# Differential attention with the scores of both maps in two row groups of TensorE, PSUM tiles of its own, and a deeper lag between scores and values

## The chip, the cores and the metric

One core of a Trainium2 chip runs the whole program. The metric is the device time of one execution in microseconds (us). TensorE (PE) multiplies, VectorE (DVE) and ScalarE (ACT) work on its results, GpSimd (POOL) and SyncE (SP) serve around them.

## What is computed

Two layers of a hybrid backbone over 256 context and 512 latent tokens. Each layer has three groups of heads (an SSD scan, differential attention, latent attention) behind one input projection, and then a mixture of 16 experts. The change is in the differential attention: four heads, each with two maps of 32 dimensions and values of 64.

```python
s1 = jnp.einsum('bqhd,bkhd->bhqk', q1, k1).astype(F32) * scale
s2 = jnp.einsum('bqhd,bkhd->bhqk', q2, k2).astype(F32) * scale
amap = jax.nn.softmax(s1, axis=-1) - lam * jax.nn.softmax(s2, axis=-1)
o = jnp.einsum('bhqk,bkhd->bqhd', amap.astype(v.dtype), v)
return rmsnorm(o, subln_w) * (1.0 - lambda_init)
```

Context queries see the 256 context keys, latent queries all 768. In layer 0 there are 2 context and 4 latent query tiles of 128 for each head, in layer 1 only the 4 latent ones.

## The kernel before

The work of the stage is cut into units, one for each head and query tile: 24 in layer 0 (8 with 256 keys, 16 with 768) and 16 in layer 1 (all with 768 keys). Everything is float32. Every engine has its own program, written out in order, and waits on semaphores; nothing is rearranged. Of each float32 matmul the trace shows two instructions, of a transpose one.

`QK` holds queries (rows m = 0, 1) and keys (m = 2, 3) with 128 partitions: four groups of 32, which are heads 2m and 2m+1, each with its two maps. To take one map alone out of the 128 partitions, ScalarE copies the queries with a mask (`split_queries`, line 821) into `QS`, so that the other 96 partitions are zero; a score matmul then runs over all 128 rows (`diff_score`, line 1568 in `scores`).

A unit on PE is (`attention`): scores of the *next* unit, both maps (512 and 256 key columns each); the transposes of this unit's weighted map, 128 columns each (`turn_tile`, line 1553); the values of the unit before (line 1579, 64 columns). VectorE (`attend`) takes the negative row maximum of each map (line 1061), combines the two exponentials (lines 1145 to 1151: the second map times its factor, added to the first) and scales the result (line 1155). ScalarE (`softmax`) computes the exponentials with their row sums (line 775) and copies the transposed map out of PSUM (line 696). The latent attention later in the layer uses the same `attention`, `softmax` and `attend` with one map.

PSUM is four tiles of 1024 columns, `ps[0]` to `ps[3]`, two banks each. Everything up to the experts goes through numbered jobs (`job_plan`, `att_job`, class `Slots`): job j uses tile j mod 4 when the job four before it has been released. The differential attention has 4 jobs for each unit (two scores, one turn, one value).

Behind the stage PE goes on with the projection for the latent attention (line 1545, 352 columns), and with the matmuls of the modulation. The latent attention's own projections use narrow matmuls: lines 1704 and 1705 (128 and 64 rows by turns, 96 columns), 1716 (32 rows and columns), 1722 (128 rows, 64 columns). In the SSD stage lines 1778 and 1812 multiply in two groups of 64 rows, into different PSUM banks.

```python
    scores(0)
    for u in range(n):
        if u + 1 < n:
            scores(u + 1)
        pe.wait_ge(*w_.next(S["prob_ready"]))
        turn_tile(...)
        if u:
            values(u - 1)
    values(n - 1)
```

## Time and profile before

| | us |
|---|---|
| median of 3 runs | 2569.79 (2564.29 to 2576.02) |
| the profiled execution | 2569.09 |
| its span on the core | 2567.3 |
| stage in layer 0, first score to last finish (146.17 to 250.35) | 104.18 |
| stage in layer 1 (1479.81 to 1561.16) | 81.35 |
| mean granted TensorE clock | 0.892 |

The profile comes from one execution. Each instruction has a start and a duration; an idle stretch is shown with the instruction that ended it. PE's matmuls are pipelined, so the duration of one is longer than its share of the engine: distances between starts tell the price. PEclk is the clock that TensorE was granted, as a share of full speed; in this trace it is at any moment either 0.50 (1.2 GHz) or 1.00 (2.4 GHz). The two stages are 7.2% of the time; the expert stages, 4 out of 10 slices and more, stream weights and are not touched.

### The profile page before, as it was taken

Reading aid. Unit: us, or ns where it says so; the run is one execution under the profiler, and the core shown is the slowest. Engines: PE = TensorE matmul, PEld = TensorE weight load, DVE = VectorE, ACT = ScalarE, POOL = GpSimd, SP = SyncE. Lnnn points to the kernel's source line nnn. Section 1 sums busy time; section 2 is a strip of 40 time slices with the busy share of each in tenths; the row PEclk is TensorE's granted clock in tenths of the full one; section 3 lists DMA queues with packets and bytes.
Section 4 is the critical chain, followed back from the end, with each engine's and each line's share of the span. In section 5 each row is a group of like instructions: output and inputs, shape, how many; then the busy total and the mean of one; then the engine's idle time right before and its main releaser. Section 6 shows DMA issues by size and latency. Waiting matters only on the chain. (4 is left out here: it accounts for less than half of the span.)

```text
span 2567.3 us, 26052 instructions
## 1 busy us (share of the span) xinstructions
PE 2187.0 (85%) x11014; PEld 1161.4 (45%) x11014; DVE 659.5 (26%) x1161; ACT 520.6 (20%) x1040; POOL 214.6 (8%) x187
## 2 busy tenths in 40 slices
PE   4898999988894999999994999999879587777774
PEld 2466456657452333333332776466544332222221
DVE  1156142127334111111103163322372400000001
ACT  3144243131230000000004252332212000000001
POOL 0000000023001111111100000000220000000000
PEclk8899889897985999999997999798869698888887
DMA  8400403100033999999996002231001599999995
GB/s 297 148 34 1 164 1 116 66 33 1 0 115 128 381 396 396 396 395 397 400 386 220 33 34 73 92 116 64 36 1 73 209 402 402 402 402 402 402 403 208
DMA packets 168647, 527.78 MB, mean 206 GB/s; under 512 B 10584, under 2 KB 24532, under 8 KB 168404
## 3 DMA queue, kind: packets, MB, share of 16 engines
q1 hardware_dynamic: 155412, 494.65, 49.6%
q0 software_dynamic: 11680, 26.22, 4.0%
q10 hardware_dynamic: 1440, 5.24, 0.5%
q8 instruction: 88, 1.44, 0.2%
q14 instruction: 27, 0.22, 0.0%
HBM read 503.02 MB, written 23.07 MB: 205 GB/s over the span
## 5 line engine op out<-in xcount | busy, mean ns | idle before, releaser
L1927 PE MATMUL ps<-ring,arena 128*64 128x512 f32 x1184 | 287.6, 640 | 56.7 <-DMA ring<-in_w_up 44.5
L1927 PE MATMUL ps<-arena 128*64 128x512 f32 x864 | 210.3, 640 | 42.5 <-DMA arena<-in_w_up 29.3
L1536 PE MATMUL ps<-arena,ring 128*128 128x256 f32 (+1 forms) x640 | 203.5, 481 | 12.3 <-DMA ring<-in_w_in 12.3
L1545 PE MATMUL ps<-ring,arena 128*128 128x256 f32 (+3 forms) x736 | 207.8, 444 | 0.0
L1927 PEld LDWEIGHTS ps<-ring,arena 128*64 128x64 f32 x1184 | 93.5, 147 | 236.4 <-issue 236.4
L696 ACT ACTIVATE arena<-ps 128x768 f32<-128x768 f32 (+8 forms) x143 | 106.9, 758 | 325.9 <-PE ps L1545 150.0
L1545 PEld LDWEIGHTS ps<-ring,arena 128*128 128x128 f32 x736 | 138.7, 215 | 67.5 <-issue 44.0
L1536 PEld LDWEIGHTS ps<-arena,ring 128*128 128x128 f32 x640 | 122.7, 192 | 92.1 <-issue 83.4
L1553 PE MATMUL ps<-const,arena 128*128 128x128 f32 x732 | 110.7, 297 | 57.9 <-ACT arena L742 38.1
L1568 PE MATMUL ps<-arena 128*128 128x256 f32 (+3 forms) x432 | 151.4, 485 | 7.6 <-ACT arena L775 4.0
L1927 PEld LDWEIGHTS ps<-arena 128*64 128x64 f32 x864 | 68.1, 147 | 173.5 <-issue 173.5
L1477 DVE TENSOR_TENSOR arena<-arena,ps 128x512 f32<-128x512 f32 x32 | 22.0, 688 | 460.4 <-ACT arena L983 460.4
L1848 PE MATMUL ps<-ring,arena 128*128 128x512 f32 x320 | 138.9, 593 | 1.1 <-DVE arena L1362 1.1
L1981 PE MATMUL ps<-ring,arena 128*64 128x512 f32 x608 | 136.8, 595 | 3.0 <-DMA ring<-in_w_down 2.3
L1553 PEld LDWEIGHTS ps<-const,arena 128*128 128x128 f32 x732 | 93.9, 155 | 80.7 <-ACT arena L742 39.7
L606 POOL DMA_INDIRECT expert_sums<-arena,small x32 | 52.8, 1650 | 865.6 <-ACT arena L990 825.1
L775 ACT ACTIVATE arena<-ps,nmax 128x768 f32<-128x768 f32 (+1 forms) x120 | 97.1, 812 | 131.4 <-DVE nmax L1061 124.7
L1061 DVE TENSOR_REDUCE nmax<-ps 128x1 f32<-128x768 f32 (+1 forms) x120 | 98.5, 846 | 69.9 <-PE ps L1568 69.9
L983 ACT ACTIVATE arena<-ps 128x512 f32<-128x512 f32 x32 | 19.1, 597 | 448.0 <-PE ps L1927 448.0
L1579 PE MATMUL ps<-arena 128*128 128x64 f32 x832 | 105.3, 277 | 0.0
L1579 PEld LDWEIGHTS ps<-arena 128*128 128x128 f32 x832 | 102.9, 199 | 0.0
L1568 PEld LDWEIGHTS ps<-arena 128*128 128x128 f32 (+1 forms) x432 | 75.9, 191 | 58.9 <-issue 50.9
(227 smaller groups left out, 2358.8 us busy)
## 6 DMA issues: line engine op xcount, KB each, us to landing
ring<-in_w_up SPq DMA_DIRECT2D x38, 2048.0 KB, 17.7
ring<-in_w_down SPq DMA_DIRECT2D x38, 2048.0 KB, 23.9
ring<-in_w_gate SPq DMA_DIRECT2D x36, 2048.0 KB, 22.5
arena<-in_w_gate SPq DMA_DIRECT2D x28, 2048.0 KB, 23.1
arena<-in_w_up SPq DMA_DIRECT2D x26, 2048.0 KB, 16.0
arena<-in_w_down SPq DMA_DIRECT2D x26, 2048.0 KB, 24.9
ring<-in_ada_w SPq DMA_DIRECT2D x24, 2048.0 KB, 13.2
ring<-in_w_in SPq DMA_DIRECT2D x6, 2048.0 KB, 9.8
```

The lines of the kernel that those rows point to most:

```text
L606: pool.indirect_dma_start(halves_sum[l], at_rows(e, 0), y_l[e % 2], None, compute_op=ALU.add)\
L696: act.activation(dst, src, func, scale=scale).then_inc(*J.free(j))
L775: act.activation(P_of[i % 2][m][:, 0:nk], J.tile(j)[:, 0:nk], ACT.Exp, bias=nmax[:, c:c + 1], accum_out=esum[:, c:c + 1]).then_inc(*J.free(j))
L1061: dve.tensor_reduce(nmax[:, c:c + 1], J.tile(j)[:, 0:nk], AX_X, ALU.max, negate=True).then_inc(S["negmax"], 1)
L1536: ins = mm(o[0:n, c0:c1], w[:, k, col:col + n], hT[:, k, c0:c1], start=k == 0, stop=k == KD - 1)
L1545: ins = mm(o[:, i * stride:i * stride + n], hT[:, k, t * P:(t + 1) * P], w[:, k, :], start=k == 0, stop=k == KD - 1)
L1553: ins = pe.transpose(o[:, k * P:(k + 1) * P], src(k), ident)
L1568: ins = mm(o[:, c0:c1], lhs, rhs, start=True, stop=True)
L1579: ins = mm(o[:, 0:64], PT_of[u % 2][:, k * P:(k + 1) * P], v_of(h, k), start=k == 0, stop=k == nk - 1)
L1848: ins = mm(o[:, hf * 512:(hf + 1) * 512], mixT[i % 2][:, k, :], wo[hf][:, k, :], start=k == 0, stop=k == KD - 1)
L1927: ins = mm(ps[0][hf * 64:hf * 64 + 64, col:col + 512], xl[e % 2][:, at:at + CAP_L], w[:, c, hf * 512:hf * 512 + 512], start=b + c == 0, st ...
L1981: ins = mm(ps[1][hf * 64:hf * 64 + 64, 512:1024], hT_l[e % 2][:, at:at + CAP_L], w[:, c, hf * 512:hf * 512 + 512], start=b + c == 0, stop= ...
```

## The change

- The masked copies and `QS` are gone. A score matmul reads 32 rows: `r` picks the row group of the head and map in `QK`, for queries and keys alike. For each span of keys the two maps follow each other, so two neighbouring matmuls stand in neighbouring row groups and write different PSUM tiles.
- The stage no longer uses the job numbering. Its scores rotate over `ps[0]` to `ps[2]` (index 2u + m modulo 3), so scores of unit u need the first exponential of unit u-1. `ps[3]` serves the rest: three transposes at a time in its first bank, the values in its second. (The number of jobs removed is a multiple of 4, so later jobs keep their tiles.)
- A tile of 768 keys is transposed and copied in two halves of 3 x 128 columns. A half waits until ScalarE has copied the one before.
- The lag is deeper: in round r PE does scores of r, then by turns halves of the transposes of r-2 and of the values of r-3. `P1` has three buffers, `P2` and `PT_d` two each, `rcol` four sets.
- Each engine has a loop of its own for the stage: `diff_softmax` on ScalarE, a loop with `diff_max`, `diff_weigh`, `diff_finish` on VectorE, and one with `diff_scores`, `diff_turn`, `diff_values` on PE. Their arithmetic is as before.

```diff
+def diff_parts(l):
+    return [(u, k, min(k + 3, n_keys(t) // P)) for u, (h, t) in enumerate(diff_units(l)) for k in range(0, n_keys(t) // P, 3)]
...
-        PD = [[ar(a2 + (2 * i + m) * TOK, TOK) for m in range(2)] for i in range(2)]
-        PT_d = [ar(a2 + (4 + i) * TOK, TOK) for i in range(2)]
-        QS = view(ar(a2 + 6 * TOK, 4 * TOK), m=4)
+        P1 = [ar(a2 + i * TOK, TOK) for i in range(3)]
+        P2 = [ar(a2 + (3 + i) * TOK, TOK) for i in range(2)]
+        PT_d = [ar(a2 + (5 + i) * TOK, TOK) for i in range(2)]
...
+                for r in range(n + 2):
+                    for m in range(2):
+                        if r >= 2:
+                            turned_out(r - 2, m)
+                        if r < n:
+                            exps(r, m)
...
-                        act.activation(QS[:, i, tq:TOK], QK[:, h // 2, tq:TOK], ACT.Copy,
-                                       scale=K[:, K_MAP + i:K_MAP + i + 1]).then_inc(S["q_split"], 1)
...
+                for r in range(n + 3):
+                    if r < n:
+                        diff_max(r, 0)
+                        diff_max(r, 1)
+                    if 1 <= r <= n:
+                        diff_weigh(r - 1)
+                    if r >= 3:
+                        diff_finish(r - 3)
...
-                def diff_score(h, m, t, c0, c1):
-                    if t == q[0] and c0 == 0:
-                        pe.wait_ge(*w_.next(S["q_split"]))
-                    return QS[:, 2 * (h % 2) + m, t * P:(t + 1) * P], QK[:, 2 + h // 2, c0:c1]
-
-                attention(l, DH, jb("datt"), 2, diff_score, PD, PT_d, lambda h, k: V[:, k, h * DV:(h + 1) * DV])
+                def diff_scores(u):
+                    h, t = units[u]
+                    if u >= 2:
+                        pe.wait_ge(S["diff_exps"], 2 * (n0 + u) - 1)
+                    elif u == 1:
+                        pe.wait_ge(S["diff_exps"], 2 * n0 + 1)
+                    for c0, c1 in spans(t):
+                        for m in range(2):
+                            r = slice(32 * (2 * (h % 2) + m), 32 * (2 * (h % 2) + m) + 32)
+                            ins = mm(ps[(2 * u + m) % 3][:, c0:c1], QK[r, h // 2, t * P:(t + 1) * P], QK[r, 2 + h // 2, c0:c1],
+                                     start=True, stop=True)
+                            if c1 == n_keys(t):
+                                ins.then_inc(S[f"diff_scored{m}"], 1)
+                def diff_turn(u, x):
...
+                    pe.wait_ge(S["diff_weighed"], n0 + u + 1)
+                    if i:
+                        pe.wait_ge(S["diff_copied"], p0 + i)
+                    for k in range(k0, k1):
+                        ins = pe.transpose(ps[3][:, (k - k0) * P:(k - k0 + 1) * P], P1[u % 3][:, k * P:(k + 1) * P], ident)
+                    ins.then_inc(S["diff_turned"], 1)
...
+                for r in range(n + 3):
+                    if r < n:
+                        diff_scores(r)
+                    for x in range(2):
+                        if 2 <= r < n + 2:
+                            diff_turn(r - 2, x)
+                        if r >= 3:
+                            diff_values(r - 3, x)
```

How PE's program reads now, at two places. The names are PSUM tile <- operands, then the shape; x3 is a count of matmuls in a row.

The start of the stage in layer 0, before: scores of line 1568 for units 0, 1 and 2, transposes of line 1553 between them.

```order
L1568 MATMUL ps1<-arena 128x256
L1568 MATMUL ps2<-arena 128x256
L1568 MATMUL ps3<-arena 128x256
L1568 MATMUL ps0<-arena 128x256
L1553 MATMUL ps1<-const,arena 128x128 x2
L1568 MATMUL ps2<-arena 128x512
L1568 MATMUL ps2<-arena 128x256
L1568 MATMUL ps3<-arena 128x512
L1568 MATMUL ps3<-arena 128x256
```

And now, where line 1740 is the scores and line 1754 the transposes.

```order
L1740 MATMUL ps0<-arena 128x256
L1740 MATMUL ps1<-arena 128x256
L1740 MATMUL ps2<-arena 128x256
L1740 MATMUL ps0<-arena 128x256
L1740 MATMUL ps1<-arena 128x512
L1740 MATMUL ps2<-arena 128x512
L1740 MATMUL ps1<-arena 128x256
L1740 MATMUL ps2<-arena 128x256
L1754 MATMUL ps3<-const,arena 128x128 x2
L1740 MATMUL ps0<-arena 128x512
```

Three units' scores (256, 256, then 512 and 256 keys) stand ahead of the first transpose, and the maps alternate within a span.

A latent unit of the same layer, before: scores of line 1568, six transposes, six values of line 1579.

```order
L1568 MATMUL ps2<-arena 128x512
L1568 MATMUL ps2<-arena 128x256
L1568 MATMUL ps3<-arena 128x512
L1568 MATMUL ps3<-arena 128x256
L1553 MATMUL ps0<-const,arena 128x128 x6
L1579 MATMUL ps1<-arena 128x64 x6
```

And now, with the values in line 1768.

```order
L1740 MATMUL ps1<-arena 128x512
L1740 MATMUL ps2<-arena 128x512
L1740 MATMUL ps1<-arena 128x256
L1740 MATMUL ps2<-arena 128x256
L1754 MATMUL ps3<-const,arena 128x128 x3
L1768 MATMUL ps3<-arena 128x64 x3
L1754 MATMUL ps3<-const,arena 128x128 x3
L1768 MATMUL ps3<-arena 128x64 x3
```

The scores are as many, the transposes and values come in threes by turns, all of them in `ps3`.

## Rows read from the trace of the kernel before

**Rows 1.** Page, first line and part 1: busy us, share of span, instructions

```profile
span 2567.3 us, 26052 instructions
...
PE 2187.0 (85%) x11014; PEld 1161.4 (45%) x11014; DVE 659.5 (26%) x1161; ACT 520.6 (20%) x1040; POOL 214.6 (8%) x187
```

**Rows 2.** Busy time by windows, both stages: stretch, us, PE, PEld, DVE, ACT, POOL, PEclk, DMA

```profile
146.17:250.35 104.18, 91.69 (x497) 68.16 (x498) 69.17 (x144) 55.25 (x124) 0.00 (x0) 0.98 0.06 21
1479.81:1561.16 81.35, 77.40 (x417) 58.87 (x418) 54.90 (x96) 43.83 (x84) 0.00 (x0) 0.96 0.08 27
```

**Rows 3.** Timeline, one latent unit of layer 1: start, us, engine, line, operation, shape

```profile
1520.10 2.80 PE L1568 MATMUL ps<-arena 128*128 128x512 f32 x8
...
1522.11 1.82 DVE L1061 TENSOR_REDUCE nmax<-ps 128x1 f32<-128x768 f32 x2
...
1522.73 0.82 PE L1553 MATMUL ps<-const,arena 128*128 128x128 f32 x6
1523.15 0.90 ACT L775 ACTIVATE arena<-ps,nmax 128x768 f32<-128x768 f32 x1 [0.79 <-DVE nmax L1061]
...
1523.39 1.45 PE L1579 MATMUL ps<-arena 128*128 128x64 f32 x12
...
1524.68 1.51 PE L1568 MATMUL ps<-arena 128*128 128x512 f32 x4
...
1524.92 0.81 ACT L696 ACTIVATE arena<-ps 128x768 f32<-128x768 f32 x1
```

**Rows 4.** Timeline of PE, three places at line 1778, 64-row matmuls

```profile
557.53 0.28 PE L1788 MATMUL ps<-const,arena 128*128 128x128 f32 x1
557.74 0.38 PE L1778 MATMUL ps<-arena 64*128 64x128 f32 x2
...
570.91 0.49 PE L1778 MATMUL ps<-arena 64*128 64x128 f32 x4 [0.16 <-ACT arena L922]
571.34 0.49 PE L1787 MATMUL ps<-const,arena 128*128 128x128 f32 x2
...
586.86 0.80 PE L1778 MATMUL ps<-arena 64*128 64x128 f32 x4
587.59 0.79 PE L1787 MATMUL ps<-const,arena 128*128 128x128 f32 x2
```

**Rows 5.** Windows again: stretches before, in and after half clock

```profile
243.40:246.60 3.20, 1.65 (x15) 1.65 (x16) 1.40 (x3) 1.20 (x2) 0.00 (x0) 1.00 0.02 5
...
1550.40:1553.90 3.50, 1.91 (x18) 1.77 (x16) 2.34 (x6) 2.57 (x5) 0.00 (x0) 1.00 0.01 2
1554.20:1560.60 6.40, 6.31 (x30) 6.32 (x31) 0.31 (x2) 0.81 (x1) 0.00 (x0) 0.50 0.01 3
298.02:322.36 24.34, 24.34 (x32) 6.27 (x32) 0.00 (x0) 2.42 (x3) 0.00 (x0) 0.50 0.47 174
322.36:331.03 8.67, 8.67 (x12) 1.56 (x11) 6.41 (x8) 0.81 (x1) 3.31 (x4) 0.50 0.00 0
...
335.40:342.00 6.60, 5.91 (x23) 3.38 (x21) 0.76 (x2) 3.92 (x5) 0.00 (x0) 1.00 0.00 0
1609.20:1626.80 17.60, 17.51 (x32) 6.30 (x32) 0.00 (x0) 1.78 (x3) 0.00 (x0) 0.50 0.63 232
...
1564.20:1572.00 7.80, 7.80 (x28) 5.05 (x27) 1.43 (x5) 0.16 (x2) 0.00 (x0) 1.00 0.00 0
```

**Rows 6.** Timeline of PE at half clock: transposes, values, 32-row and 64-column matmuls

```profile
1554.29 1.54 PE L1553 MATMUL ps<-const,arena 128*128 128x128 f32 x6 [1.98 <-DVE arena L1151]
1555.62 5.22 PE L1579 MATMUL ps<-arena 128*128 128x64 f32 x24
1560.63 1.49 PE L1545 MATMUL ps<-ring,arena 128*128 128x352 f32 x2
...
322.36 8.74 PE L1716 MATMUL ps<-arena,const 32*32 32x512 f32 x10
331.03 7.50 PE L1722 MATMUL ps<-arena,w_kv_up 128*64 128x512 f32 x16
```

More of the change, by code:

```diff
@@ L148, in job_plan, with diff_units, diff_before, diff_parts_before @@
     return at
+def diff_units(l):
+    return [(h, t) for h in range(DH) for t in query_tiles(l)]
+def diff_before(l):
+    return sum(len(diff_units(i)) for i in range(l))
+def diff_parts(l):
+    return [(u, k, min(k + 3, n_keys(t) // P)) for u, (h, t) in enumerate(diff_units(l)) for k in range(0, n_keys(t) // P, 3)]
+def diff_parts_before(l):
+    return sum(len(diff_parts(i)) for i in range(l))
 def att_job(base, maps, n, u, kind, m=0):
@@ L760, in conditioning, with diff_softmax, exps, turned_out @@
                 modulation(l, 0)
+            def diff_softmax(l):
+                units, parts, n0, p0 = diff_units(l), diff_parts(l), diff_before(l), diff_parts_before(l)
+                n = len(units)
+                def exps(u, m):
+                    nk, c = n_keys(units[u][1]), 2 * (u % 2) + m
+                    act.wait_ge(*a.next(S["negmax"]))
+                    if m == 0:
+                        if u >= 3:
+                            act.wait_ge(S["diff_turned"], p0 + len([p for p in parts if p[0] <= u - 3]))
+                        if u >= 2:
+                            act.wait_ge(S["diff_weighed"], n0 + u - 1)
+                    act.activation((P1[u % 3] if m == 0 else P2[u % 2])[:, 0:nk], ps[(2 * u + m) % 3][:, 0:nk], ACT.Exp,
+                                   bias=nmax[:, c:c + 1], accum_out=esum[:, c:c + 1]).then_inc(S["diff_exps"], 1)
+                def turned_out(u, x):
+                    mine = [(i, p) for i, p in enumerate(parts) if p[0] == u]
+                    if x >= len(mine):
+                        return
+                    i, (_, k0, k1) = mine[x]
+                    if x == 0 and u >= 2:
+                        act.wait_ge(S["diff_valued"], n0 + u - 1)
+                    act.wait_ge(S["diff_turned"], p0 + i + 1)
+                    act.activation(PT_d[u % 2][:, k0 * P:k1 * P], ps[3][:, 0:(k1 - k0) * P], ACT.Copy)\
+                        .then_inc(S["diff_copied"], 1)
+                for r in range(n + 2):
[4 more added lines that the diff above has]
+                            exps(r, m)
             def softmax(l, heads, base, maps, P_of, PT_of, after_exps=None):
@@ L1140, in _, with diff_max @@
                     dve.wait_ge(*v.next(S["qk_roped"]))
[L1142 to L1145 removed]
+                units, n0 = diff_units(l), diff_before(l)
+                n = len(units)
+                def diff_max(u, m):
+                    nk, c = n_keys(units[u][1]), 2 * (u % 2) + m
+                    dve.wait_ge(S[f"diff_scored{m}"], n0 + u + 1)
+                    if u >= 2:
+                        dve.wait_ge(S["diff_exps"], 2 * (n0 + u - 2) + m + 1)
+                    dve.tensor_reduce(nmax[:, c:c + 1], ps[(2 * u + m) % 3][:, 0:nk], AX_X, ALU.max,
+                                      negate=True).then_inc(S["negmax"], 1)
@@ new lines, in _ @@
+                n = len(units)
+                def diff_scores(u):
+                    h, t = units[u]
+                    if u >= 2:
+                        pe.wait_ge(S["diff_exps"], 2 * (n0 + u) - 1)
[8 more added lines that the diff above has]
+                                ins.then_inc(S[f"diff_scored{m}"], 1)
@@ new lines, in diff_turn @@
+                def diff_turn(u, x):
+                    mine = [(i, p) for i, p in enumerate(parts) if p[0] == u]
+                    if x >= len(mine):
+                        return
+                    i, (_, k0, k1) = mine[x]
+                    pe.wait_ge(S["diff_weighed"], n0 + u + 1)
[4 more added lines that the diff above has]
+                    ins.then_inc(S["diff_turned"], 1)
@@ new lines, in diff_values @@
+                def diff_values(u, x):
+                    h, t = units[u]
+                    mine = [(i, p) for i, p in enumerate(parts) if p[0] == u]
+                    if x >= len(mine):
+                        return
+                    i, (_, k0, k1) = mine[x]
+                    pe.wait_ge(S["diff_copied"], p0 + i + 1)
+                    if x == 0 and u:
+                        pe.wait_ge(S["diff_finished"], n0 + u)
+                    last = n_keys(t) // P
+                    for k in range(k0, k1):
+                        ins = mm(ps[3][:, 512:512 + DV], PT_d[u % 2][:, k * P:(k + 1) * P], V[:, k, h * DV:(h + 1) * DV],
+                                 start=k == 0, stop=k == last - 1)
+                    if k1 == last:
+                        ins.then_inc(S["diff_valued"], 1)
```

51 lines of the change are left out of this document (24 added, 27 removed).

## The prediction

> **What bounds the kernel now.** TensorE is busy 85% of the span [rows 1], so I first cut out the two stretches that hold the changed stage, by stage windows: layer 0 takes 104.18 us with PE busy 91.69, layer 1 81.35 us with PE busy 77.40, the clock at 0.98 and 0.96 of full; the queue of work behind them is PE's next projection, so what they gain or lose goes into the total one to one [rows 2]. Then the order in time of one steady unit (layer 1, a latent tile with 768 keys) [rows 3]: scores start at 1520.10, transposes at 1522.73, values at 1523.39, the next scores at 1524.68. That is 2.63 + 0.66 + 1.29 = 4.58 us with PE never waiting; 16 units make 73.3 of the 81.35 us. VectorE is busy 54.90/16 = 3.4 us and ScalarE 43.83/16 = 2.7 us a unit [rows 2]. PE is the bound, at the full clock of 2.4 GHz.
>
> **The change part by part.**
>
> *Scores by row groups.* Each matmul of the scores now reads 32 rows, and the two maps stand in neighbouring row groups and in different PSUM tiles. The nearest row is the pair of 64-row matmuls of line 1778: four take 0.43 us from load to the next full-array load (570.91 to 571.34), and the first two together span 0.38 us, one lone full-array matmul and a load of 0.1 us (0.28 at 557.53) [rows 4]. So pairs do run side by side. For a latent unit this makes 2.56 us of streams (2.63 less the first load) into 1.28 us.
>
> *Going in and out of row groups.* Full-array matmuls of 128 columns follow each other 0.11 us apart (six transposes in 0.66 us [rows 3]), but line 1788 to line 1778 takes 0.21 us, and a visible load of about 0.1 us follows; four 64-row matmuls should stream in 2 x 0.11 us and take 0.43, so 0.2 us goes on the way out [rows 4]. One visit costs 0.4 us at the full clock; at half clock 0.73 less 2 x 0.21 leaves 0.3, plus the turn-in and its load again 0.3: 0.6 us. Bounds are 0.3 and 0.6 there. I take 0.6, since the stage visits just as line 1778 does, between full-array work.
> The rule for this stands in the Trainium skill, "TensorEngine Tiling (Array Packing)", Key Properties: a change of tiling mode drains the engine. The trace agrees with 0.2 us each way; a sum that left it out would be 24 us lower for 40 visits.
>
> *PSUM and order.* Three score tiles instead of four slots: scores of unit u wait for the first exponential of unit u-1. Before, the first two units' scores stood in a row; now each of the first rounds is scores, a wait for maximum and exponential, scores. Behind the waiting scores stand the transposes of u-2 and values of u-3, and ScalarE's copy of them. Copies by halves: 0.81 us for 768 columns becomes two of about 0.5 (an estimate between zero saving and twice 0.81), on ScalarE, which has 1.9 us free. The masked copies of line 821 (8 in all, about 0.7 to 0.9 us each) go from ScalarE; they hid behind PE, so nothing is won. The VectorE work is the same.
>
> *Would the loop hold 4.58 at full clock?* Scores to availability 0.2 + 1.28 + 0.27, maximum 0.95 (two in 1.82), ScalarE ready only after the half copy of the tile turned in between (about 0.15 late), exponential with its accumulator 1.0: 3.9 us a unit. PE's own sum is 1.28 + 0.4 + 0.66 + 1.29 = 3.63, so that loop would be the bound. It would still be a gain. But it needs 2.4 GHz.
>
> **The clock decides.** What the engine did before its clock fell: 1.65 us of work in 3.20 (243.4 to 246.6), and 1.91 in 3.50 (1550.4) [rows 5]; both are waits for VectorE in the stage's own tail, and both are followed by half clock, 1.2 GHz. The new stage opens like that: in layer 1 its first two rounds each hold 1.5 us of score matmuls in a round of about 3.6 us (latencies as above), and these fill 64 of the 128 rows. I expect the clock to fall there, in both layers.
>
> Before, full-array work brought it back: after some us of line 1545, which begins at 1560.63 [rows 6], the clock is 1.00 from 1564.2 [rows 5]. In the new stage two kinds of work alternate, and each has a row in which a busy PE did **not** bring it back [rows 5]. Matmuls on 64, 96 or 128 rows by turns and then on 32 rows (lines 1704, 1705, 1716) fill PE without a gap from 298.02 to 331.03, 33 us, and again from 1609.20, and the clock is 0.50 throughout; behind them the 128-row matmuls of line 1722, which begin at 331.03 [rows 6], raise it (1.00 from 335.4). Transposes and values (lines 1553, 1579) fill 6.31 of 6.40 us from 1554.20 at 0.50. PE being busy was not enough in either. With scores on 64 of 128 rows and transposes and values between them I expect the clock to stay at 0.50 to the stage's end.
> The Trainium skill, "TensorE: Matmul & The Clock Gate", What's actually happening, says that activity releases the throttle, and its advice is to keep PE busy without long gaps. By that alone a PE with 3.63 us of work in 3.9 is safe; that is rival A below, 2554 us. The 33 us above speak against it.
>
> **The sum at half clock.** Prices by rows at 0.50: ten 32-row matmuls of 512 columns in 8.67 us (322.36 to 331.03), 0.86 each; six transposes in 1.33 us (1554.29 to 1555.62, 0.16 of it a first load), so about 0.213 each; 24 value instructions in 5.01 us (1555.62 to 1560.63), 0.209 each [rows 6]. A latent unit: scores 2 x 0.86 + 2 x 0.43 = 2.58, visit 0.6, transposes 6 x 0.213 = 1.28, values 12 x 0.209 = 2.51: 7.0 us. PE is then far behind every other engine and hides all their waits.
> Layer 0: scores 16 x 2.58 + 8 x 0.86 = 48.2; visits 24 x 0.6 = 14.4; 112 transposes 23.9; 224 value instructions 46.8; sum 133.3. Opening and tail: before, 81.35 - 73.3 = 8 us in layer 1; now a round more at the front, less what the first 5 us at full clock save. I take 9 here and 6 in layer 1. Layer 0: 142.3, **+38.1**.
> Layer 1: 16 x 2.58 + 16 x 0.6 + 96 x 0.213 + 192 x 0.209 = 111.4, with 6: 117.4, **+36.1**.
> The profiled execution took 2569.09 us (span 2567.3 and 1.8 around it), 0.7 below the median of three, 2569.79. 2569.1 + 74.2 = **2643 us**. Bounds: visits at 0.3 take 12 off, opening and tail give or take 8, projection still at half clock after the stage adds up to 4.
>
> **Rivals.**
> A. *The clock holds* (it never falls, or comes back within some us). Units of 3.9 us: layer 1 16 x 3.9 + 9 = 71, layer 0 16 x 3.9 + 8 x 3.2 + 6 = 94, and 3 us in each for one dip at the start or end: 97 and 74, so -7 and -7: **2554 us** (2549 to 2560). For it: PE's gaps stay short, 0.98 now. Against: rows 5. Chance 0.13.
> B. *The clock falls and comes back now and then*, for example at the context tiles, where full-array work of older units stands closer together: half way, about **2600 us**. Chance 0.10.
> C. *The row groups run one after the other*, since each float32 matmul is two instructions and the second pass could block the neighbour. Then scores double at half clock, +48 and +41 on the above: **2732 us**; at full clock units of 4.6 to 5.0 and +18, 2587. Against: line 1778 is float32 too, and its pairs lie together [rows 4]. Chance 0.05.
> The side on which it turns slower: from about 15% of the stage at half clock on, the 15 us of rival A are eaten (a unit at half clock costs 3.1 us more; 5 of 40 units do it).
>
> **How the numbers follow.** Forecast 0.72, A 0.13, B 0.10, C 0.05. The predicted time is the forecast's. The range takes it with its bounds (2620 to 2672) and B: 2575 to 2675, 0.81. About 0.5% (13 us) is what a measurement of this kernel can tell from no change; faster by more is most of A, 0.10; within it the rest of A and the edge of B, 0.04; slower 0.86.
>
> **What would show it.** The granted clock of the two stretches: 0.5 and a stage of about 142 and 117 us, against 0.95 and 97 and 74. Score matmuls in pairs that start together, four pairs in 2.6 us at half clock; a unit of 7.0 us in layer 1; VectorE and ScalarE waiting for PE. Elsewhere every stage should last as long as before. I am wrong if the clock treats two maps side by side as it treated the full-array scores, if the opening is denser than I think so that the clock never falls, or if pairs don't form.

## The result and the profile after

| | before | changed |
|---|---|---|
| median, us | 2570.89 (2564.29 to 2576.02, 4 runs) | 2622.18 (2617.97 to 2629.14, 4 runs) |
| span of the profiled execution, us | 2567.3 | 2618.4 |
| stage in layer 0, us | 104.18 | 134.86 |
| stage in layer 1, us | 81.35 | 111.98 |
| mean granted clock | 0.892 | 0.853 |

The changed kernel takes 1.0204 times the time of before, 95% interval 1.017 to 1.0237: slower by 51 us. In its text the scores stand on line 1740, the transposes on 1754, the values on 1768; the maxima are line 1187, the weighing lines 1195 to 1200, the finish 1206, the exponentials 794, the copies out of PSUM 805. The projection behind the stage, line 1545 before, is line 1603.

The page of the changed kernel, its first line, the first line of part 1 and the clock row of part 2 (tenths of full speed in 40 slices):

```profile
span 2618.4 us, 26071 instructions
...
PE 2243.1 (86%) x11014; PEld 1195.2 (46%) x11014; DVE 656.9 (25%) x1161; ACT 514.8 (20%) x1056; POOL 215.1 (8%) x187
...
PEclk8865879988895999999997956799879688888888
```

Against [rows 1], PE has the same number of matmuls and is busy 56 us longer; the work of VectorE and ScalarE is almost the same. The two stages by windows, and in layer 1 the two parts of its opening and the rest (columns as in [rows 2]: stretch, us, busy time of PE, PEld, DVE, ACT and POOL, granted clock, DMA share, GB/s):

```profile
145.62:280.48 134.86, 127.88 (x497) 91.48 (x498) 68.47 (x144) 54.92 (x136) 0.00 (x0) 0.52 0.05 16
1505.42:1617.40 111.98, 106.66 (x417) 77.82 (x418) 54.67 (x96) 44.17 (x96) 0.00 (x0) 0.51 0.06 19
...
1505.42:1508.41 2.99, 1.56 (x8) 0.74 (x8) 1.36 (x2) 0.36 (x1) 0.00 (x0) 1.00 0.90 264
1508.41:1516.94 8.53, 5.78 (x16) 2.35 (x16) 3.59 (x6) 3.38 (x8) 0.00 (x0) 0.50 0.40 153
1526.00:1617.40 91.40, 90.93 (x362) 68.85 (x362) 43.45 (x79) 35.24 (x78) 0.00 (x0) 0.50 0.00 1
```

Where [rows 2] read 0.98 and 0.96, these read 0.52 and 0.51. In layer 1 the clock falls 3.0 us after the first score. The last row is the one to keep: PE is busy 90.93 of 91.40 us and stays at half clock, 1.2 GHz, for all of it. The timeline of PE, first the opening of layer 1, then a steady unit (start, us, engine, line, shape, how many; in brackets the idle time before and what ended it):

```profile
1505.42 1.56 PE L1740 MATMUL ps<-arena 32*128 32x512 f32 x8 [0.78 <-ACT arena L715]
1509.09 2.93 PE L1740 MATMUL ps<-arena 32*128 32x512 f32 x8 [2.11 <-ACT arena L794]
1514.09 2.93 PE L1740 MATMUL ps<-arena 32*128 32x512 f32 x8 [2.07 <-ACT arena L794]
...
1532.68 2.93 PE L1740 MATMUL ps<-arena 32*128 32x512 f32 x8
1535.54 0.90 PE L1754 MATMUL ps<-const,arena 128*128 128x128 f32 x3
1536.24 1.38 PE L1768 MATMUL ps<-arena 128*128 128x64 f32 x6
1537.41 0.85 PE L1754 MATMUL ps<-const,arena 128*128 128x128 f32 x3
1538.05 1.38 PE L1768 MATMUL ps<-arena 128*128 128x64 f32 x6
1539.36 2.93 PE L1740 MATMUL ps<-arena 32*128 32x512 f32 x8
```

The opening holds 1.56 us of scores, a wait of 2.11 us for the exponential (line 794), and scores again, now at 2.93 us: the same eight instructions at half the clock. The kernel before had more work and a shorter wait in that place:

```profile
1479.81 5.40 PE L1568 MATMUL ps<-arena 128*128 128x512 f32 x16 [0.84 <-issue]
1486.29 0.87 PE L1553 MATMUL ps<-const,arena 128*128 128x128 f32 x6 [1.07 <-DVE arena L1151]
```

The steady unit runs from 1532.68 to 1539.36, 6.68 us, with no wait; the unit of [rows 3] took 4.58. VectorE and ScalarE now wait for PE: the waits in the stage of layer 0 (engine, line, what it waited for; total us, times, longest) begin with

```profile
ACT arena L805 <- PE ps L1754: 73.7, 40, 3.8
DVE nmax L1187 <- PE ps L1740: 57.1, 24, 17.2
```

**Where the 51.1 us of span come from.** The stages give 30.7 and 30.6. The rest gives back 10.2: 0.6 before the first stage, 4.5 between the stages (2567.3 being cut at 250.35 and 1479.81 before, at 280.48 and 1505.42 now) and 5.1 behind the second. No code changed there. The stretches at half clock fall in other places: added up over these three parts they make 542 us before and 529 us in the changed kernel. If 12 us more at full clock save half their length, that is 6 of the 10.2 us, an estimate; the rest stays open, and runs of the kernel before alone lie up to 12 us apart. One half-clock stretch in layer 0 of the kernel before, then a longer window of the changed one that takes in the same matmuls, some 25 to 30 us later and at full clock (the 64-row matmuls at 586.86 in [rows 4] begin at 612.31 here):

```profile
577.70:591.30 13.60, 13.60 (x61) 10.45 (x60) 8.10 (x10) 1.02 (x1) 4.43 (x4) 0.50 0.00 1
```

```profile
593.60:620.90 27.30, 21.66 (x180) 18.74 (x180) 20.20 (x24) 6.95 (x18) 16.92 (x12) 1.00 0.01 1
```

The middle and the end moved in the experiments too, whatever was edited: the middle lay between 1223.3 and 1233.5 us and the end between 1000.3 and 1006.6. So totals carry some 10 us of this, and the stage's own length is the better witness.

### The profile page after: what moved, and what is told of

Same layout as the page of the kernel before. It is cut to its first block and busy times, and to the rows that moved or that the text cites. A ratio compares the mean times of both kernels' runs of the same rounds, so it can differ in the third digit from the quotient of the medians.

```text
span 2618.4 us, 26071 instructions
## 1 busy us (share of the span) xinstructions
PE 2243.1 (86%) x11014; PEld 1195.2 (46%) x11014; DVE 656.9 (25%) x1161; ACT 514.8 (20%) x1056; POOL 215.1 (8%) x187
## 5 line engine op out<-in xcount | busy, mean ns | idle before, releaser
L2036 PE MATMUL ps<-arena 128*64 128x512 f32 x864 | 210.8, 641 | 41.3 <-DMA arena<-in_w_up 28.1
L1603 PEld LDWEIGHTS ps<-ring,arena 128*128 128x128 f32 x736 | 137.8, 214 | 66.8 <-issue 43.2
L715 ACT ACTIVATE arena<-ps 128x768 f32<-128x768 f32 (+8 forms) x103 | 78.0, 773 | 328.7 <-PE ps L1603 157.4
L1611 PE MATMUL ps<-const,arena 128*128 128x128 f32 x524 | 80.7, 306 | 46.4 <-ACT arena L761 39.1
L1740 PE MATMUL ps<-arena 32*128 32x256 f32 (+1 forms) x288 | 100.6, 840 | 12.2 <-ACT arena L794 10.7
L1611 PEld LDWEIGHTS ps<-const,arena 128*128 128x128 f32 x524 | 70.2, 160 | 61.5 <-ACT arena L761 40.3
L1768 PEld LDWEIGHTS ps<-arena 128*128 128x128 f32 x416 | 96.7, 333 | 2.1 <-issue 2.1
L1768 PE MATMUL ps<-arena 128*128 128x64 f32 x416 | 96.3, 406 | 0.9 <-DVE arena L1206 0.9
L2090 PE MATMUL ps<-arena 128*64 128x512 f32 x416 | 93.6, 594 | 1.3 <-DMA arena<-in_w_down 1.3
L1957 PEld LDWEIGHTS ps<-ring,arena 128*128 128x128 f32 x320 | 60.2, 190 | 74.3 <-issue 72.7
L1187 DVE TENSOR_REDUCE nmax<-ps 128x1 f32<-128x768 f32 (+1 forms) x80 | 64.3, 846 | 113.0 <-PE ps L1740 113.0
```

The lines of the kernel that those rows point to most:

```text
L715: act.activation(dst, src, func, scale=scale).then_inc(*J.free(j))
L1187: dve.tensor_reduce(nmax[:, c:c + 1], ps[(2 * u + m) % 3][:, 0:nk], AX_X, ALU.max, negate=True).then_inc(S["negmax"], 1)
L1603: ins = mm(o[:, i * stride:i * stride + n], hT[:, k, t * P:(t + 1) * P], w[:, k, :], start=k == 0, stop=k == KD - 1)
L1611: ins = pe.transpose(o[:, k * P:(k + 1) * P], src(k), ident)
L1740: ins = mm(ps[(2 * u + m) % 3][:, c0:c1], QK[r, h // 2, t * P:(t + 1) * P], QK[r, 2 + h // 2, c0:c1], start=True, stop=True)
L1768: ins = mm(ps[3][:, 512:512 + DV], PT_d[u % 2][:, k * P:(k + 1) * P], V[:, k, h * DV:(h + 1) * DV], start=k == 0, stop=k == last - 1)
```

## The experiments

Theory: the row groups and the order do what they should, and the loss is the clock. The thin opening drops it to half, and the narrow work does not bring it back. Rivals: the new order and PSUM layout cost the time; the row groups run one after the other; steady scores on 32 rows pull the clock down by themselves. The total of each run is a median, and one execution of each kernel was profiled. The stages of all kernels, from the profiled executions (ratio against the kernel before on the same chip):

| kernel | ratio, 95% | layer 0, us, clock | layer 1, us, clock |
|---|---|---|---|
| before | 1 | 104.2, 0.98 | 81.3, 0.96 |
| changed | 1.0204 (1.017 to 1.0237) | 134.9, 0.52 | 112.0, 0.51 |
| e1_full_rows | 1.0003 (0.9987 to 1.0018) | 104.4, 1.00 | 84.5, 1.00 |
| e2_rows_only | 1.0301 (1.0263 to 1.0338) | 147.5, 0.51 | 112.1, 0.51 |
| e3_opening_filled | 1.0037 (1.0019 to 1.0055) | 134.1, 0.54 | 68.9, 1.00 |
| e4_maps_in_turn | 1.0246 (1.0201 to 1.0291) | 135.5, 0.51 | 112.1, 0.52 |
| e5_rows64 | 0.9887 (0.9846 to 0.9928) | 91.1, 0.98 | 68.9, 1.00 |
| e6_latents_first | 0.9893 (0.986 to 0.9927) | 87.7, 0.93 | 70.2, 1.00 |
| e7_filled_more | 1.0022 (1.0003 to 1.0041) | 122.7, 0.64 | 70.2, 1.00 |
| e8_order_alone | 1.0251 (1.0218 to 1.0284) | 133.1, 0.52 | 112.0, 0.52 |
| e9_contexts_filled | 0.9901 (0.9869 to 0.9933) | 92.3, 0.98 | 70.2, 1.00 |
| e10_burst_inside | 1.0125 (1.0093 to 1.0157) | 133.8, 0.58 | 87.0, 0.80 |

### e1_full_rows: the new order with scores on 128 rows

```diff
-                            r = slice(32 * (2 * (h % 2) + m), 32 * (2 * (h % 2) + m) + 32)
+                            r = slice(0, P)
```

> The changed kernel with one edit: scores run over all 128 rows instead of 32, in the new order and the new PSUM layout (the queries are not masked, so a score sums over both maps and two heads: the output is not the reference's, the shapes and the instructions are). Theory 1, the slowdown is the clock, and it is the 32-row scores that hold it down: the clock falls at the openings, comes back within some us, and both stages run mostly at full clock; scores take 2.56 us again, no visits to row groups, units of 4.6 to 4.8 us, stages of about 112 and 88 us, against 134.9 and 112.0 in the changed kernel: 2618 - 47 = about 2573, near the kernel before. Rival, it is the waits of the new order that hold the clock down, whatever the rows: half clock stays, scores cost 5.1 us a unit, stages of 180 and 150 us, about 2700.

Measured: 2566.53 us, ratio 1.0003. By windows, both stages:

```profile
144.55:248.99 104.44, 92.14 (x498) 68.02 (x499) 68.03 (x144) 53.86 (x136) 0.00 (x0) 1.00 0.06 21
1478.71:1563.17 84.46, 77.41 (x418) 56.46 (x419) 53.57 (x96) 42.63 (x96) 0.00 (x0) 1.00 0.08 26
```

The opening has the changed kernel's order with somewhat shorter waits (1.72 and 1.64 us against 2.11 and 2.07), and with full rows the clock does not fall at all; a dip had been expected, with stages of 112 and 88 us. All ten runs have a mean clock of 0.892 to 0.894. The order and the PSUM layout cost 3 us in layer 1, and about nothing in layer 0. All of the loss hangs on what scores on 32 rows bring with them. Waits of 1.6 to 1.7 us in rounds of 4.5 us did not drop the clock here; but PE also works longer in these rounds (2.8 us, since nothing runs side by side), so this run does not yet tell rows from busy time. Its first rounds in layer 1:

```profile
1478.71 2.82 PE L1740 MATMUL ps<-arena 128*128 128x512 f32 x8 [0.78 <-ACT arena L715]
1483.24 2.85 PE L1740 MATMUL ps<-arena 128*128 128x512 f32 x8 [1.72 <-ACT arena L794]
1487.73 2.85 PE L1740 MATMUL ps<-arena 128*128 128x512 f32 x8 [1.64 <-ACT arena L794]
```

### e2_rows_only: the old order and PSUM with scores on 32 rows

The kernel before with 32-row scores, its maps by turns for each span of keys, and no masked copies. The four slots of the job numbering, whole transposed tiles and the shorter lag stay:

```diff
-                        for c0, c1 in spans(t):
+                    for c0, c1 in spans(t):
+                        for m, j in enumerate(js):
...
-                    return QS[:, 2 * (h % 2) + m, t * P:(t + 1) * P], QK[:, 2 + h // 2, c0:c1]
+                    r = slice(32 * (2 * (h % 2) + m), 32 * (2 * (h % 2) + m) + 32)
+                    return QK[r, h // 2, t * P:(t + 1) * P], QK[r, 2 + h // 2, c0:c1]
```

> The kernel before with the row groups alone: old order, old PSUM jobs, whole-tile transposes; scores on 32 rows, the maps by turns within a span, no masked copies. Theory 1 (32-row scores at half the rows don't bring the clock back, and PE waits at the start let it fall): half clock through both stages, units of 6.7 us, stages of about 135 and 112 us, about 2620. Rival, the deeper lag with its thin opening makes the clock fall, and the old order, which starts with two units' scores in a row, keeps it: full clock, units of 4.0 to 4.3 us, 2555 to 2565.

Measured: 2643.87 us, ratio 1.0301, stages 147.5 and 112.1 us at clock 0.51. Scores on 32 rows drop the clock in the old order as well. They also thin its opening: in layer 1 it holds 2.95 us of scores and then a wait of 3.25 us for VectorE, against 5.40 and 1.07 us before, so this run does not part rows from busy time either. Given half clock, the new order is worth 12.6 us in layer 0 (147.5 against 134.9) and nothing in layer 1. The 135 us expected for layer 0 missed this: PE is idle for 18.5 us of the stage here (busy 128.95 of 147.48) and for 7.0 us in the changed kernel.

### e3_opening_filled: idle full-array matmuls in the first two rounds

```diff
                     if r < n:
                         diff_scores(r)
+                    if r < 2:
+                        for _ in range(2):
+                            mm(ps[3][:, 0:512], QK[:, 2, 0:P], QK[:, 2, 0:512], start=True, stop=True)
```

> The changed kernel with two idle full-array matmuls of 512 columns behind the scores of the first two units of each layer (they write the unused PSUM tile 3, nobody reads them), which fill PE's waits at the opening. They cost at most 4 x 0.85 us a layer where PE would work, nearly nothing where it waits. Theory 1: the fall at the opening is what starts the half clock; in layer 1 the clock then holds for some or all of the stage (units of 3.9 us, stage of 71 to 75 us instead of 112.0), in layer 0 it falls again at a round behind the context tiles, where little full-array work stands beside the scores, and stays down (stage 125 to 140 us). 2575 to 2590. Rival: steady units with row-group scores can't hold the clock either, so it falls a few us later, and the time is that of the changed kernel, 2618 to 2625.

Measured: median 2577.83 us of ten runs, of which seven took 2574 to 2581 us and three 2621 to 2624; the ratio of 1.0037 is that of the seven. The timeline of PE in layer 1, opening and two steady units:

```profile
1504.23 1.56 PE L1740 MATMUL ps<-arena 32*128 32x512 f32 x8 [0.78 <-ACT arena L715]
1505.72 1.98 PE L1778 MATMUL ps<-arena 128*128 128x512 f32 x4
1507.90 1.56 PE L1740 MATMUL ps<-arena 32*128 32x512 f32 x8 [0.20 <-ACT arena L794]
...
1518.92 1.56 PE L1740 MATMUL ps<-arena 32*128 32x512 f32 x8
...
1522.76 1.56 PE L1740 MATMUL ps<-arena 32*128 32x512 f32 x8
```

The fillers (line 1778) stand in time that was idle: the wait for the exponential shrinks from 2.11 us to 0.20. Layer 1 then holds the full clock to its end and takes 68.9 us (71 to 75 were expected), against 112.0 and against 81.3 before; a unit takes 3.84 us. So the whole change is worth 12 us in this stage once the clock stands; against e1, which has the new order too, the row groups with these fillers are worth 15.6 (84.5 to 68.9). In layer 0 the clock fell at 155.3, within the first rounds. Two of them are context units with a third of a latent unit's score columns, and e7, with more fillers, gets past this place. The three longer runs lie some 45 us above the others, about the 43 us that layer 1 gained. Their mean granted clock was 0.851 to 0.855, that of the seven 0.871 to 0.873. A layer 1 at half clock, some 113 us in the changed kernel, makes 113 x 0.5 / 2620 = 0.022 of the mean: the size fits, though no trace of these three was taken.

### e4_maps_in_turn: all of one map, then all of the other

```diff
-                    for c0, c1 in spans(t):
-                        for m in range(2):
+                    for m in range(2):
+                        for c0, c1 in spans(t):
```

> The changed kernel with the two loops of the scores swapped: first both spans of map 0, then both of map 1. Theory 1 with pairs made by neighbours in the program: only the middle two matmuls lie side by side, so at half clock a unit's scores take 0.85 + 0.43..0.85 + 0.43..0.85, about 4.3 us instead of 2.56, 32 latent units are 1.7 us longer: about 2670. Rival: PE starts the other row group's work early whatever stands between, and the time stays at 2620.

Measured: 2629.70 us (two runs), stages 135.5 and 112.1: as the changed kernel. I had thought that the second matmul of map 0, on the same row group as the first, would hold up map 1 behind it. The line of the scores asked in two short windows (duration in ns least/median/most, first and last start, shapes), around 230.25 and around 231.1:

```profile
L1740 PE MATMUL ps<-arena x4: 1056/1138/1218, 229.3 to 230.3; 32*128 32x512 f32 x4
...
L1740 PE MATMUL ps<-arena x4: 629/842/1057, 230.3 to 231.1; 32*128 32x512 f32 x2, 32*128 32x256 f32 x2
```

A float32 matmul is two instructions, so the four of 512 columns are those of both maps. They all start by 230.3, and the first of 256 columns at 231.1. In the program map 0's 256 columns stand ahead of map 1's 512. Pairs form across the row groups out of the program's order, and the order in which the maps are written does not matter here. The Trainium skill, "TensorE: Matmul & The Clock Gate", The mechanism, says that matmuls start in program order without reordering; for two row groups these rows show otherwise, and the measurement decides.

### e5_rows64: two row groups of 64 rows

```diff
-                            r = slice(32 * (2 * (h % 2) + m), 32 * (2 * (h % 2) + m) + 32)
+                            r = slice(64 * m, 64 * m + 64)
```

Each score here sums two maps' dimensions; the time is that of the same number of matmuls with the whole array in use.

> The changed kernel with one edit: the scores of map 0 run over rows 0 to 63 and those of map 1 over rows 64 to 127, still two row groups side by side, the same number, order, columns and PSUM tiles (the sums run over both maps of a head, so the output is not the reference's). Theory 1, few active rows hold the clock down: with two groups of 64 the whole array is in work. The clock may dip at the openings, but comes back within some us and holds: stages of 94 to 100 us and 70 to 76 us instead of 134.9 and 112.0, total 2550 to 2565. Rival 1: row groups as such (or the visits and gaps they bring) hold it down, whatever their height: half clock, 2618 to 2630. Rival 2, the thin opening alone: it falls and stays down here too, 2618 to 2630.

Measured: 2535.36 us, ratio 0.9887. By windows, both stages, then in layer 0 the one stretch at half clock and what follows:

```profile
144.32:235.44 91.12, 74.52 (x498) 52.67 (x499) 67.55 (x144) 55.02 (x136) 0.00 (x0) 0.98 0.07 24
1458.71:1527.63 68.92, 60.65 (x418) 44.31 (x419) 53.49 (x96) 43.63 (x96) 0.00 (x0) 1.00 0.09 32
147.90:151.30 3.40, 3.31 (x10) 1.48 (x10) 0.93 (x3) 0.49 (x3) 0.00 (x0) 0.50 0.85 327
151.30:235.44 84.14, 69.80 (x482) 50.60 (x481) 64.92 (x137) 52.98 (x128) 0.00 (x0) 1.00 0.00 1
```

The opening of layer 1 on PE:

```profile
1458.71 1.56 PE L1740 MATMUL ps<-arena 64*128 64x512 f32 x8 [0.78 <-ACT arena L715]
1462.39 1.56 PE L1740 MATMUL ps<-arena 64*128 64x512 f32 x8 [2.11 <-ACT arena L794]
1466.02 1.56 PE L1740 MATMUL ps<-arena 64*128 64x512 f32 x8 [2.07 <-ACT arena L794]
```

Same instructions, same order, and to the digit the same waits of 2.11 and 2.07 us as in the changed kernel, with twice the rows: the clock does not fall. Only one execution was traced, but the mean clock of all four is 0.887 to 0.899, against 0.849 to 0.853 in the changed kernel. This is the sharpest comparison of the study: at the opening of layer 1, at equal busy time, the rows in use decide.

In layer 0, whose first rounds are shorter, 64 rows do not keep the clock up: it falls at 147.9. It is back at 151.3 with 64-row pairs running, while the changed kernel, once down, stayed down for 133 us. At that place the two differ in busy time too, since the fall comes at another point of the round. PE is busy 3.31 of 3.40 us in e5, and in the changed kernel

```profile
150.00:153.00 3.00, 2.26 (x8) 0.70 (x6) 1.34 (x2) 0.70 (x2) 0.00 (x0) 0.50 0.67 253
```

For the way back the comparison is therefore the steady loop of the changed kernel: 90.93 of 91.40 us busy and no rise, where e5 rose within 3.4 us. The stages came out shorter than expected (94 to 100 and 70 to 76 us), and so did the total.

What is in the rows does not seem to matter: the kernel before also multiplies 32 rows of queries at a time, with zeros in the other 96, and stood at 0.98 and 0.96. What no run parts is the number of rows from the row groups of 32 as such; four of them at once, with all 128 rows in use, were not tried.

### e6_latents_first, e7_filled_more, e8_order_alone: what layer 0 needs

e7 fills more of the opening (the last two parts of the diff); e8 puts the 16 latent units ahead of the 8 context units (the first part); e6 does both.

```diff
-    return [(h, t) for h in range(DH) for t in query_tiles(l)]
+    return [(h, t) for late in (False, True) for h in range(DH) for t in query_tiles(l) if (t < CT) == late]
...
+                    if u == 0 and x == 0:
+                        mm(ps[3][:, 576:1024], QK[:, 2, 0:P], QK[:, 2, 0:448], start=True, stop=True)
...
+                    for _ in range((2, 2, 1)[r] if r < 3 else 0):
+                        mm(ps[3][:, 512:1024], QK[:, 2, 0:P], QK[:, 2, 0:512], start=True, stop=True)
```

> The changed kernel with two edits, meant to be faster than both: (a) in both layers PE's waits of the first rounds are filled with idle full-array matmuls (2, 2 and 1 of 512 columns behind the scores of units 0, 1, 2, and one of 448 ahead of the first values), into banks of PSUM tile 3 that nobody reads; (b) all latent units come before all context units. Theory 1: the clock holds through the 16 latent units in both layers (3.9 us each) and falls only in the 8 context units of layer 0, which cost 2.5 to 2.8 us each at half clock: stages of 89 to 94 and 70 to 74 us, against 104.2 and 81.3 before, total 2541 to 2551. Rival: the clock falls in the steady latent units of layer 0 as it did in the run with two fillers: stage of 115 to 130 us, total 2575 to 2590.

> The same fillers in both layers, with the units in the changed kernel's order (context tiles at the start of each head). Theory 1, rounds behind the context tiles have too little full-array work beside their narrow scores: layer 0 falls there and stays at half clock (stage 125 to 138 us), layer 1 holds in every run (70 to 74 us): 2570 to 2582, without the runs at 2622 that the version with fewer fillers had in 3 of 10. Rival: layer 0 fell only because its opening was thin; with more fillers it holds as well, stage of 96 to 100 us, total 2548 to 2556.

> The changed kernel with the latent units first and no filler. Theory 1: the opening of layer 0 is now that of layer 1, thin, so the clock falls in both and stays down: stages of 130 to 136 and 112 us, 2615 to 2622. Rival: the context tiles at the start were what let it fall in layer 0, and with latent units first it holds there: stage of 90 to 95 us, 2575 to 2582.

Measured: e6 2539.76 us, ratio 0.9893; e7 2572.25, 1.0022; e8 2629.65 (two runs), 1.0251. The windows of layer 0, e7 up to where its clock fell and behind it, and then e6 from where its clock fell:

```profile
144.06:178.30 34.24, 29.28 (x170) 18.15 (x172) 23.98 (x53) 19.59 (x51) 0.00 (x0) 1.00 0.18 62
178.30:266.72 88.42, 86.55 (x341) 63.80 (x340) 44.25 (x92) 35.25 (x86) 0.00 (x0) 0.50 0.00 1
```

```profile
219.80:232.24 12.44, 11.16 (x45) 8.56 (x44) 6.91 (x24) 4.65 (x17) 0.00 (x0) 0.50 0.00 1
```

With more filler e7 gets past the opening, and the clock falls at 178.3 instead. PE's timeline of e7 there:

```profile
174.39 1.56 PE L1740 MATMUL ps<-arena 32*128 32x512 f32 x8 [0.41 <-ACT arena L794]
175.88 0.44 PE L1754 MATMUL ps<-const,arena 128*128 128x128 f32 x2
176.15 0.56 PE L1770 MATMUL ps<-arena 128*128 128x64 f32 x4
178.01 2.70 PE L1740 MATMUL ps<-arena 32*128 32x512 f32 x8 [1.31 <-ACT arena L794]
```

These are the rounds in which latent scores meet the transposes and values of a context unit: 1.00 us of full-array work beside 1.56 us on 32 rows, and a wait of 1.31 us. Once down, it stays down for 88 us, since the steady units do not raise it. Each head brings such a place. Putting the latent units first leaves them at the end of the stage, where only 12.4 us are left (e6: 87.7 us, where 89 to 94 were expected). The order alone, with the opening unfilled, gives nothing (e8: 133.1), because the clock is down at 149.9, in the scores of the second latent unit; its total of 2629.65 us is 8 us above the expected range though both stages are in theirs (133.1 and 112.0 us): the middle took 1233.2 us in it and 1224.9 in the changed kernel. e6 computes the same as the changed kernel and takes 2539.76 us against 2568.76 before on the same chip, 1.1% less: it is the correct kernel that keeps what the row groups save. e7's layer 0 took 122.7 us, a little less than the expected 125 to 138.

### e9_contexts_filled: and the context rounds of e6 filled too

```diff
+                    for _ in range(1 if t < CT else 0):
+                        mm(ps[(2 * u) % 3][:, 0:448], QK[:, 2, 0:P], QK[:, 2, 0:448], start=True, stop=True)
                     for c0, c1 in spans(t):
```

> The kernel with fillers and latent units first, and one idle full-array matmul of 448 columns ahead of the scores of each of the 8 context units of layer 0 (it writes the score tile that the real scores then overwrite). In the trace of that kernel the clock stood at full from 144 to 219.8 us and fell there, among context rounds in which the engine waited 0.59 us for an exponential in rounds of 2.1 us; 12.4 us of the stage and 4.8 us of the projection behind it ran at half clock. Theory (thin rounds start the half clock): the filler closes these gaps, the clock stays at 1.00 to the stage's end, layer 0's stage takes 84 to 87 us in place of 87.7, and the total is 2533 to 2538 against 2539.8. Rival (the context rounds are too thin with a filler too, or the clock falls for another reason): a fall again near 220 to 228, the fillers cost up to 3 us, 2541 to 2545. Layer 1 has no context units: 70.2 us, clock 1.00, in both.

Measured: 2541.30 us, ratio 0.9901. The clock now holds through the context rounds and falls at 232.1, 3.6 us ahead of the end, behind a wait of 0.93 us for VectorE in the stage's tail. The context rounds have the same wait for the exponential as in e6 (0.59 and 0.60 us) and more full-array work, which speaks for the theory's cause. But the stage takes 92.3 us and not 84 to 87. In PE's timeline there:

```profile
221.89 1.02 PE L1738 MATMUL ps<-arena 128*128 128x448 f32 x2 [0.60 <-ACT arena L794]
222.84 0.70 PE L1742 MATMUL ps<-arena 32*128 32x256 f32 x4
...
224.90 1.02 PE L1738 MATMUL ps<-arena 128*128 128x448 f32 x2 [0.60 <-ACT arena L794]
```

The wait of 0.60 us for the exponential is as long as ever, and the filler stands behind it, ahead of the scores: a context round takes 3.0 us in place of 2.1. Eight times 0.9 is 7 us, more than the half clock had cost. I had taken the filler for one that fills the gap; it leaves the gap and adds its own time. In the profiled executions the middle, which no edit touched, hides this in the total: 1225.9 us here and 1233.4 in e6.

### e10_burst_inside: six full-array matmuls in the middle of the half clock

The opening is as in the changed kernel.

```diff
+                    for _ in range(6 if u == 6 else 0):
+                        mm(ps[(2 * u) % 3][:, 0:512], QK[:, 2, 0:P], QK[:, 2, 0:512], start=True, stop=True)
                     for c0, c1 in spans(t):
```

> The changed kernel, and six idle full-array matmuls of 512 columns in a row ahead of the scores of unit 6 of each layer, inside the half clock stretch; nothing in the opening. It asks whether the scores on 32 rows keep the clock down by themselves, or only fail to raise it. Theory (they only fail to raise it: once up, steady units of latent tiles hold it): in layer 1 the clock falls at about 1508 as before, the burst begins near 1539 and takes about 5 us, the clock reads 1.00 from within it to the stage's end, 10 units take 3.9 in place of 6.7 us, and the stage takes about 88 to 90 us in place of 112.0. In layer 0 unit 6 is a context unit with another behind it; the clock comes up there and falls again at that or the next pair of context units: 120 to 138 us in place of 134.9. Total 2590 to 2605. Rival (steady scores on 32 rows pull the clock down again in any case, and the kernel with a filled opening held it for a reason of its own): clock 0.50 again a few us behind the burst, layer 1 about 115 us, total 2625 to 2632.

Measured: 2600.71 us, ratio 1.0125. Layer 1 by windows, from the fall to the burst, and from the rise to the end, and PE's timeline around the burst:

```profile
1510.80:1542.27 31.47, 27.40 (x100) 18.00 (x101) 17.34 (x29) 14.29 (x31) 0.00 (x0) 0.50 0.13 51
1545.00:1595.47 50.47, 47.74 (x320) 34.79 (x319) 35.44 (x66) 29.00 (x64) 0.00 (x0) 1.00 0.00 1
```

```profile
1535.73 2.93 PE L1742 MATMUL ps<-arena 32*128 32x512 f32 x8
...
1542.27 6.71 PE L1738 MATMUL ps<-arena 128*128 128x512 f32 x12
1548.91 1.56 PE L1742 MATMUL ps<-arena 32*128 32x512 f32 x8
...
1552.75 1.56 PE L1742 MATMUL ps<-arena 32*128 32x512 f32 x8
```

The unit ahead of the burst runs at half clock (2.93 us of scores, 6.5 us to the burst), the units behind it at the full one, 3.84 us from 1548.91 to 1552.75, and so to the stage's end: 87.0 us, where 88 to 90 were expected. The same instructions in the same order keep either level. So steady 32-row scores with full-array work between them neither raise the clock nor pull it down. The rival that they pull it down is out. In layer 0 the clock rose at 172.8 and fell again at 189.9, in the rounds behind a pair of context units, and the stage took 133.8: the rises and falls are where the theory puts them.

## Why the prediction was right

The forecast was 2643 us in a range of 2575 to 2675, by the clock falling in the openings and staying down; measured were 2622.18. By its own steps:

- **The clock.** It fell 4.3 us into the stage of layer 0 and 3.0 us into that of layer 1, and stayed down to 283.0 and 1621.1, in the projection behind each. e3 shows that the opening is what drops it in layer 1, and e10 that the steady units do not; e5 and e10 show what brings it back, and e5 that the rows and not the waits alone decide. The reading of [rows 5], that a busy PE can stay at half clock when its matmuls are narrow, was what told this from rival A. It holds for 91.4 us here. The likeness was loose, though: the matmuls of lines 1704 and 1705 use 128 and 64 rows (the 96 are columns) and those of line 1716 only 32 columns, while the scores use all 128 columns. The Trainium skill, "TensorE: Matmul & The Clock Gate", What's actually happening, has activity release the throttle. By the trace being busy is not enough for that: PE was busy 90.93 of those 91.40 us.
- **The unit at half clock.** 6.68 us against 7.0. From start to start, the scores take 2.86 (their first load and the way out of the row groups included), the transposes 0.70 + 0.64 = 1.34 (1.28 in the sum) and the values 1.17 + 1.31 = 2.48, the way into the row groups included (2.51). With the terms of the sum for scores, transposes and values (2.58 + 1.28 + 2.51 = 6.37), 0.31 is left for the visit, where I took 0.6. The term was mis-sized: I had chosen the upper of its two bounds, and the lower one, 0.3, held. (The 0.213 for a transpose is right, but (1.33 - 0.16) / 6 is 0.195: of the first start distance, 0.27 us, only 0.05 is extra.) Part of the 0.6 is one load counted twice: at line 1778 the first pair starts at 586.86 and the second at 587.23, 0.16 us more than the 0.21 of a pair, so the 0.3 left over there already held the load that was added again. The 0.3 too much makes 24 x 0.3 = 7 us in layer 0, which is nearly all of 142.3 against 134.9, and 16 x 0.3 = 5 us in layer 1, nearly all of 117.4 against 112.0.
- **Openings and tails.** With the visits at 0.3 what is left of my 9 and 6 us is right within a microsecond.
- **Outside the stages.** "Elsewhere every stage should last as long as before" was off by 10.2 us. Half-clock stretches that moved explain some 6 of them by the estimate above, and the rest is open. Together with 12.8 us in the two stages that makes the 23 us between 2643 and the profiled execution's span of 2618.4 with 1.8 around it.
- **Pairs (rival C).** They form: eight score instructions take 2.93 us at half clock and 1.56 at full. C is out, and e4 shows that they form even where the program puts the maps one behind the other.
- **The loop at full clock (rival A).** 3.9 us a unit were worked out, 3.84 measured in e3 and e10; layer 1 takes 68.9, where 71 and a dip stood in the sum. A's price was right, its condition was not met.
- **Rival B.** It let the clock come back at the context tiles. The opposite is so: those rounds are where it falls (178.3 in e7, 219.8 in e6, 189.9 in e10), because a context unit's transposes and values are few beside 32-row scores and PE waits there for exponentials.
- **What I had not separated.** I laid the fall to the opening's waits and mentioned the narrow rows beside them. e5, with the same waits in layer 1 and 64 rows a matmul, does not fall: there it takes both. By the busy time that I compared, 1.65 in 3.20 and 1.91 in 3.50 us, e5's layer 1 with 1.56 in 3.68 should have fallen as well. So the fall was forecast from a measure that is not enough, and its coming true owes something to luck.

## What to carry to other kernels

Two score maps side by side on 32 rows each took 1.56 us a unit where the same matmuls on 128 rows took 2.8 (e3, e1), but they leave 64 of the 128 rows in use. So look at the granted clock of the stage before counting the gain: in layer 1 the change gave 12 us at the full clock (e3) and cost 31 us at half. If the clock falls at the opening, look for waits there and put idle full-array matmuls into them, not ahead of useful work, and put the rounds with the least full-array work last, so that a fall has little left to slow. This is what e3, e6 and e9 show for one kernel. Compare stages and not totals when the clock moves, since stages that nobody touched change by some microseconds with it.

## What the hardware showed that I had not expected

- The same steady loop of 32-row scores, transposes and values holds both levels: 0.50 for 91.4 us in the changed kernel, 1.00 for 50.5 us behind the burst of e10. One burst of 6.6 us changes the following 50.
- With 64-row pairs PE came back to the full clock by itself (e5, half from 147.9 to 151.3 us); with 32-row pairs it stayed down for 91.4 us of nearly gapless work, to the projection behind the stage.
- Matmuls on different row groups start out of the program's order: in e4 all four instructions of 512 columns start by 230.3 us, ahead of those of 256 columns at 231.1 that stand before two of them in the program.
- Going in and out of row groups leaves a unit at half clock about 0.3 us longer than the sum of its matmuls, for 2.9 us of scores.
- One kernel can stand on the edge: e3 took 2574 to 2581 us in seven runs and 2621 to 2624 us in three.
